# Sample rows join 96 prompt rows in the even portion of a hybrid decoder step, and the cache attention moves there

## The reference, cut to what matters

```
h  = rmsnorm(x) @ w_in                         # split into u, v, value and gate of glu, q, three gates
A  = gelu(u) * (tril(w_s) @ layernorm(gelu(v)) + b)       # in chunks of 128 rows; a sample chunk has 4 rows
B  = silu(layernorm(causal_depthwise_conv(glu, 31 taps))) # a sample starts from its conv state
M  = softmax(q @ mem_k) @ mem_v                # 4 heads of 256, 256 memory rows
x += (sig(gA) * (A @ w_oA) + sig(gB) * (B @ w_oB) + sig(gM) * (M @ w_oM)) @ w_out
x += peer(rmsnorm(x))     # 8 heads x top 16 of 128 x 128 product keys: dots with gathered u rows,
                          # then a weighted sum of the gathered v rows
```

## Time and profile before

| | |
|---|---|
| median of 3 runs | 2285.58 us (2284.76 to 2286.41) |
| profiled execution, its time | 2276.99 us |
| its span, first to last instruction | 2275.3 us |
| PE, DVE, ACT, POOL busy | 1634.6, 1574.6, 662.4, 669.7 us |
| moved by DMA | 895.53 MB, mean 394 GB/s |
| mean granted tensor clock | 0.798 |

### The profile page before, as it was taken

One profiled execution on the slowest core, in us unless ns is written; L12 is line 12 of the kernel. 1 busy time (PEld: TensorE's weight loads), 2 busy tenths in 40 slices (PEclk: granted clock), 3 DMA queues, 4 the chain that ended last, 5 costly groups with the idle time before them and its releaser, 6 DMA issues.

```text
span 2275.3 us, 31198 instructions
## 1 busy us (share of the span) xinstructions
PE 1634.6 (72%) x10876; PEld 1059.8 (47%) x10876; DVE 1574.6 (69%) x4199; ACT 662.4 (29%) x1662; POOL 669.7 (29%) x596
## 2 busy tenths in 40 slices
PE   8999977579897567788889647776999853334333
PEld 8865665357775145454534414643877620000001
DVE  3545288779756676877675567967865677776875
ACT  2112234321423242332123223342123233322222
POOL 0000032323332342333223233221322344444442
PEclk9999999779997678898889757877989865555555
DMA  8676899999999999999999999999999999999997
GB/s 297 267 289 251 295 391 421 420 421 408 412 420 420 421 421 420 422 401 417 421 381 423 421 421 409 415 409 406 414 375 412 392 393 422 422 421 421 421 421 310
DMA packets 127100, 895.53 MB, mean 394 GB/s; under 512 B 16065, under 2 KB 16897, under 8 KB 19169
## 3 DMA queue, kind: packets, MB, share of 16 engines
q0 software_dynamic: 83232, 604.02, 64.4%
q1 hardware_dynamic: 43712, 289.53, 31.9%
HBM read 885.38 MB, written 8.11 MB: 393 GB/s over the span
## 4 chain that ended last, share of the span: by engine, by line
DMA 34%; PE 29%; DVE 20%; issue 7%; ACT 4%; DVEq 3%; POOL 2%; SPq 0%; POOLq 0%; ACTq 0%
DMA uv<-uv_in,idx_u 24%; PE bank L1499 13%; DVE uv L1378 9%; DMA ring<-w_in 5%; PE bank L2005 4%; DMA ring<-cache_in 4%; PE bank L1505 4%; PE bank L1754 4%; DVE yB L964 3%; POOL uv L506 2%; DVEq L959 1%; ACT diag L881 1%; ACT L558 1%; DVE x L1399 1%; DVE pick L1343 1%
## 5 line engine op out<-in xcount | busy, mean ns | idle before, releaser
L506 POOL DMA_INDIRECT uv<-uv_in,idx_u x574 | 654.3, 1140 | 1381.0 <-PE bank L2005 933.4
L1378 DVE CUSTOM_DVE_ANT_0 uv<-uv,xrep 128x1024 f32<-128x1024 f32 x576 | 681.1, 1220 | 213.5 <-DMA uv<-uv_in,idx_u 211.9
L2005 PE MATMUL bank<-uv,diag 128*32 128x512 f32 x2176 | 401.0, 819 | 467.8 <-ACT diag L881 464.8
L1499 PEld LDWEIGHTS bank<-xnT,ring 128*128 128x128 f32 x3200 | 442.3, 204 | 81.2 <-issue 69.7
L1499 PE MATMUL bank<-xnT,ring 128*128 128x160 f32 (+1 forms) x3200 | 464.1, 306 | 6.7 <-DMA ring<-w_in 5.2
L558 ACT ACTIVATE pick<-pick 128x2 f32<-128x2 f32 (+1 forms) x324 | 69.6, 215 | 1062.0 <-DVE pick L1378 1061.4
L2005 PEld LDWEIGHTS bank<-uv,diag 128*32 128x32 f32 x2176 | 50.5, 124 | 658.3 <-ACT diag L881 594.9
L964 DVE SCALAR_TENSOR_TENSOR yB<-ext_p,small,yB 128x128 f32<-128x128 f32 x960 | 277.3, 350 | 20.4 <-issue 1.1
L558 ACT ACT_TABLE_LOAD x140 | 179.6, 1283 | 2.5
L881 ACT ACTIVATE diag<-gated_fold,pick 128x32 f32<-128x32 f32 x576 | 153.7, 314 | 9.6 <-ACT pick L558 0.2
L1754 PE MATMUL bank<-ring,xnT 128*128 128x512 f32 x192 | 89.6, 622 | 0.0
(11 more groups left out here) (228 smaller groups left out, 1769.9 us busy)
## 6 DMA issues: line engine op xcount, KB each, us to landing
ring<-w_in SPq DMA_DIRECT2D x216, 1024.0 KB, 9.8
ring<-cache_in SPq DMA_DIRECT2D x32, 1024.0 KB, 17.8
uv<-uv_in,idx_u POOLq DMA_INDIRECT x578, 16.4
uv<-w_in SPq DMA_DIRECT2D x4, 1024.0 KB, 13.4
ext_s<-state_in SPq DMA_DIRECT2D x2, 1088.0 KB, 13.7
convs_out<-ext_s SPq DMA_DIRECT2D x2, 1088.0 KB, 31.1
ext_s<-mem_in SPq DMA_DIRECT2D x2, 1024.0 KB, 14.9
memk_out<-phase SPq DMA_DIRECT2D x2, 1024.0 KB, 11.8
```

What stands on the lines that cost most here:

```text
L506: nc.gpsimd.indirect_dma_start(out=uvbuf[2 * b + i], out_offset=None, in_=uv_in, in_offset=bass.IndirectOffsetOnAxis(ap=ids[:, c:c + 1], a ...
L1378: ins = V.tensor_tensor_reduce(out=u, in0=u, in1=xrep[gg % 2][:, :], scale=1.0, scalar=0.0, op0=ALU.mult, op1=ALU.add, accum_out=hid[:, c: ...
L1499: ins = MM(out, w[:, k, P * b:P * (b + 1)], rhs(k), start=k == 0, stop=k == KB - 1)
L2005: ins = MM(vbank[gg % 2][c:c + 32, :], diag[:, t % 4, i], uvbuf[2 * b + i][:, D + 512 * n:D + 512 * (n + 1)], start=first, stop=last)
```

## The change

- The 32 sample rows go to the even portion, ahead of 96 prompt rows, so it has 128 columns as before. The odd portion has 160 prompt rows and no sample rows. The last 32 of them stand in the extra columns.
- The samples' convolution (state load, sample taps, store of the new state), their attention to the cache (ck, cv, sk, pts, sv, ot) and the store of their normalised v rows move to the even portion, with orders rewritten for all engines. There, q comes first, each mk or mv piece is followed by two cache pieces, and the prompt's own attention comes behind mv and sv, between the va pieces.
- In the odd portion the prompt's attention gets a fifth item for the 32 extra rows, all four heads in one (S4, T4, O4). The convolution runs over 160 columns there and over 96 in the even portion. The taps of the odd portion are handed out anew: three at each of the eight first mg places.
- A chunk of 128 rows of the spatial gate now lies across both portions. The masks are 160 columns wide, and the even portion keeps a partial sum (spart) for the odd one.
- The piece ua0 is kept for the odd portion like va3. The kept pieces now lie in the memory's and in the conv state's buffers, and are loaded when these come free.
- The expert scores have 9 slots instead of 10.

```diff
-SCORE_SLOTS = 10
+SCORE_SLOTS = 9
+SEQ_COLS = (slice(T_S, P), slice(0, P + T_S))
+SEQ_N = (P - T_S, P + T_S)
 def items(m):
+    kinds = [("glu", 0, 8), ("q", 0, 4)]
     if m % 2 == 0:
-        kinds = [("glu", 0, 8), ("mk", 0, 1), ("q", 0, 1), ("mk", 1, 2), ("q", 1, 2), ("mk", 2, 3), ("q", 2, 3), ("mk", 3, 4),
-                 ("mv", 0, 1), ("q", 3, 4), ("mv", 1, 4), ("va", 0, 4)]
-    else:
-        kinds = [("glu", 0, 8), ("q", 0, 4), ("va", 0, 3), ("ck", 0, 8), ("va", 3, 4), ("cv", 0, 8)]
+        for j in range(4):
+            kinds += [("mk", j, j + 1), ("ck", 2 * j, 2 * j + 2)]
+        for j in range(4):
+            kinds += [("mv", j, j + 1), ("cv", 2 * j, 2 * j + 2)]
+    kinds += [("va", 0, 4)]
...
-KEPT = [("va", 3)]
+KEPT = [("va", 3), ("ua", 0)]
...
     if p == 0:
...
+        out += some("q", h, *range(4))
+        out += some("mk", kv, 0) + some("sk", 2, 0, 1) + some("mk", kv, 1) + some("sk", 2, 2, 3)
+        out += some("mk", kv, 2) + some("pts", 0.8, 0) + some("sk", 2, 4, 5) + some("mk", kv, 3) + some("sk", 2, 6, 7)
+        out += some("mv", kv, 0) + some("pts", 0.8, 1) + some("sv", 2, 0, 1) + some("mv", kv, 1) + some("sv", 2, 2, 3)
+        out += some("mv", kv, 2) + some("sv", 2, 4, 5) + some("mv", kv, 3) + some("sv", 2, 6, 7)
+        out += some("va", across, 0) + S(0) + S(1) + [("ot", 0.8)] + some("va", across, 1) + T(0) + S(2) + some("va", across, 2)
+        out += T(1) + S(3) + T(2) + some("va", across, 3) + O(0) + O(1) + T(3) + O(2)
     else:
...
+        out += some("q", h, 0) + S(0) + some("q", h, 1) + S(1) + some("q", h, 2) + T(0) + S(2) + some("q", h, 3) + T(1) + S(3)
+        out += some("va", across, 0) + S(4) + O(0) + T(2) + some("va", across, 1) + O(1) + T(3) + some("va", across, 2) + O(2) + T(4)
+        out += some("va", across, 3) + O(3) + some("mg", h / 2, 0) + O(4) + some("mg", 3 * h / 2, 1)
...
-                    if p == 1 and (kind, i) == ("q", 3):
+                    if (kind, i) == ("q", 3):
                         sp.wait_ge(S["glu"], at("glu", m, 8))
...
# the even portion, vector engine
+                    yield from beside("q1", 1)
...
+                    yield from beside("mk0", 3)
...
+                    yield from beside("mv1", 4)
...
# the even portion, scalar engine: the exponentials stand behind the copies of mk2 and mv0
+                    for i in range(3):
+                        yield from mk(i)
+                    weigh_sample(0)
+                    yield from turned_sample(0)
+                    yield from mk(3)
+                    yield from mv(0)
+                    weigh_sample(1)
...
# the odd portion, vector engine
+                    yield from beside("va3", 3)
+                    yield from beside("O3", 2)
-                    yield from gated(0, 3, 2)
+                    yield from gated(0, 3, 3)
                     yield from norm_v_gain()
-                    yield from gated(3, 5, 2)
+                    yield from gated(3, 5, 3)
                     yield from norm_v_bias()
-                    yield from gated(5, 8, 2)
+                    yield from gated(5, 8, 3)
...
# convolve
+                            out, seq = yB[:, c, SEQ_COLS[p]], ext_p[:, c, w:w + SEQ_N[p]]
```

521 lines of the change are left out of this document (284 added, 237 removed).

## The result

After the change: 2317.40 us, median of 4 runs (2317.10 to 2318.67), against 2285.99 us for the kernel before on the same chip (2284.76 to 2288.14). The ratio is 1.0137, 95% interval 1.0120 to 1.0155: slower by 31 us. In two later sessions, on chips 2 and 13, the same kernel gave 1.0185 (1.0159 to 1.0211) and 1.0176 (1.0152 to 1.0201), some 40 us more than before. The forecast was +10.5 us. The direction was right, the size was not.

What follows compares the result with a forecast made beforehand. Tensor engine bounds up to the first gather, then the DMA stream, with the vector engine near it at the odd taps; +24 - 46.5 + 33 = +10.5 us, median 2296 us, range 2266 to 2320 (the forecast's own 2284 to 2310).

Steps and rivals of the forecast that it cites:

- Part 1: Stage before the first gather: layer 0's cache attention moves where the tensor engine binds and is paid, +24 us (17 to 32).
- the stated 0 to 4: First stage: possible waiting of 0 to 4 us for the cache pieces, requested at 355 GB/s with stores beside.
- Part 4: Costs nothing: even taps, extra prompt-row work, split-chunk copies, 9 score slots, later EARLY pieces, masks, stores of normalised rows.
- Part 2: Behind the first gather: 19.6 MB fewer bytes in the DMA stream, -46.5 us.
- Part 3: Odd portions: vector work of the taps exceeds DMA time and leaves DMA idle, +33 us (6 to 55).
- an excess of 36 to 38 us: Odd portions: vector time over DMA time from S4 to mg9, 36 and 38 us; the slots hide 15 to 17.
- what these places lose now: Odd portions before the change: 3.3 and 4.1 us of existing DMA loss, 7 in all, deducted from the added idleness.
- the 1.8 us of Part 4: Odd portion: time of O4's products, the out product for the last 32 prompt rows, taken to lie under the stream.
- (c): Rival: hard first stage, ring behind at mk and ck, +32, vector part at its upper bound; +40, 2326 us, chance 0.10.
- (a): Rival: odd portions' vector excess is hidden; -16, 2270 us, chance 0.24.
- (b): Rival: the edits cancel, 10 us more hidden in each stretch; 0, 2286 us, chance 0.16.
- (d): Rival: first-stage cache products hidden behind pieces the tensor engine would wait for anyway; given nothing of its own.

Runs made afterwards that it cites:

- e1: Changed kernel with the four early weight loads each issued behind a mixing load (mg12 to mg18) instead of all ahead of ua1; 1.0120 of the kernel before.
- e2: Changed kernel with 8 of each odd portion's tap steps moved from mg0 to mg7 into the glu phase; 1.0070 of the kernel before.
- f2: Changed kernel with one product of 256 columns in place of O4's 16 small ones, run beside a control; 1.0150 of the kernel before.
- e3: Changed kernel with 23 of the 62 tap steps of each odd portion left out; 0.9989 of the kernel before.
- e11: Changed kernel with e1, e2, e6, three more tap steps moved from va3 and O3 to glu, planner's cost of O4 5 instead of 1.2; 0.9973 of before.
- e4: Changed kernel with the planner's costs from va0 to sg3 of the odd portions 1.3 times as large; 1.0184 of the kernel before.
- e6: Changed kernel with 8 odd-portion tap steps moved from mg0 to mg7 to mg8 to mg11, csum and csq later; 1.0099 of the kernel before.
- f5: e11 plus cache-score turns one product pair later and one tap step fewer at each spatial product, one more at mg8 to mg11; 0.9957 of before.

## Why the prediction was right in sign and wrong in size

**Part 1, +24 (17 to 32) for the first stage: it was +41.5.** The walk up to gt0 was nearly right, 23.3 forecast for its terms and 28.2 measured; 3.4 of the rest is short waits for the ring, inside the stated 0 to 4, of which the sum took 0.4. What failed is a sentence of Part 4: the EARLY pieces "are fetched later, at ua0 instead of mv0, but over 100 us ahead of their first use", counted as nothing. It asked when the pieces are wanted, and not what stands behind them in the queue. ua1's load stood there: 4.36 us of waiting and 2.3 us at the lower level behind it, and e1 gets 6.7 us back with that one edit. The second step that failed is the clock, which has no term. The earlier trace rows showed 0.99 for a stage with hardly a wait, and it was taken to stay; the stage ran at 0.96. Rows at the lower level add some 6 us beside ua1's: O1 and O2 1.9, gt0 0.9, gt2 2.3 and the rows from 304.06 on 1.3. Part of them follows waits. gt2's does not: it is there in all six profiles without ua1's wait, and absent in two with it (e2 and f2). It stands behind the spatial products; why the level falls there is open.

**Part 2, -46.5: right.** 19.8 MB less. The even portion 2 kept 1.01 in the window shown, but not to its end: at 1148 us, in its knot of the prompt's attention, one window has 0.84, where the kernel before has none below 0.95 between 307 and 1587 us. That gap of 3 us is small, and it is one for which the forecast saw no cause.

**Part 3, +33 (6 to 55): it was +46.5, inside the bounds.** The mechanism was right: vector busy 0.89, gathers released late, dots never idle. The size of a step was right (37 against 34 ns for the width), and e3's 62% and e2's 57% are near the share that an excess of 36 to 38 us less 15 to 17 hidden leaves (57%), though the spread of the marks is wide. One reading was not: for the odd portion of layer 1 "what these places lose now" was taken from 1380 to 1500 us. Its first mg products stand from 1587 us on, and from 1560 to 1700 us the kernel before already ran at 394 GB/s, a loss of 9 us against 421.5 and not of 4. Two couplings are missing. One is O4: the 1.8 us of Part 4 measured 7.04, and 3.65 at full clock, in a corner where TensorE had waited 10.5 us. Without it some 6 us come back (5.9 by the ratios, not clear of the noise), in the second odd portion alone. The other is the granularity: the excess was summed over the whole stretch and set against slots, but slots are refilled one pair's values at a time, and in the corner two intervals of 14 to 17 us between values (va3 to mg1) meet a queue that brings no piece of the ring. e11 changes only where the pairs stand; it splits one of the two, and the corner's gap in the first odd portion all but closes. That e4, which leaves them as long, gains nothing fits this; it is not shown to be the reason. e2 and e6 take steps out of mg0 to mg7, and their gain needs no more than the excess.

**Part 4.** Right for the score slots, the masks, the copies and the even portions' taps, as far as no wait in the profile names them; not tried one by one. Wrong for EARLY and O4.

**Sum.** +10.5 became +41.6 by the span: +17.5 from the first stage and +13.5 from behind the first gather. The base makes a small difference more: the ratios of three sessions give 31 to 42 us.

**Rivals.** The text's own test, "if the first gather comes after 320 us (then c)", came true at 328.46. (c) had the ring behind at mk and ck; the ring did fall behind, but at ua1, and behind the first gather nearly the upper bound holds, as (c) has it. Its 2326 is 9 us above the result, and near what the ratios of the two later sessions give; the forecast's 2296 is 21 below. (a) is excluded by the share of 0.79 to 0.87, and (b) by the interval. (d) was rightly given nothing.

**What stays open.** How much of the first stage's +41.5 needs to stay: f5 still has its first gather 29 us later than before, of which some 16 are the cache's products and their turns. What takes the first stage's clock down at the spatial products. And the cause of the window some 800 us behind the first gather (0.82 in f5, 0.75 to 0.89 in the other versions).

## What to carry to other kernels

When a transfer is moved in a queue, price what stands behind it at the new place, not only the date of its own use. Where one engine's order interleaves long auxiliary work with the short work that frees a buffer, look at the longest intervals between two releases and at what else the queues can bring in them, not only at the sum over the stretch. Moving tap steps to places where the vector engine had room, spreading the early loads aside, with one planner cost took 42 us off the time behind the first gather, nearly as much as the bytes saved (46.5). And take a stage's granted clock as something that the change may move: here it fell behind waits of 4 to 10 us, and also at gt2, where there was none.

## What the runs showed of the hardware

- After a wait of 10.1 us TensorE did the next 8 value products in 1.94 us instead of 1.06, and the 16 gate products that followed 9 us later in 3.87 instead of 2.34. After waits of 3.75 to 5.01 us, 64 products took 8.75 to 10.33 us in eleven profiles, and 7.31 in the six without a wait.
- The clock also fell without a wait: in e1, after 42 us in which TensorE was busy without a gap and which end with the spatial products, the next 3.9 us were granted 0.50, and 16 products took 9.94 us instead of 7.13. The same place is slow in 15 of 17 profiles.
- 32 products of 32 columns, each with its own 128 x 128 weights, take 7.04 us at the lower level and 3.65 at the higher, 114 ns each. 32 products of 128 columns take 3.84 there: at so few columns the width no longer sets the time.
- A load of 1 MB that was issued behind five others on one queue was there 18.2 us after its issue, where the median of the kernel before is 4.9.
- The same kernel stands at 1.0137, 1.0176 and 1.0185 of its predecessor in different sessions, and its first gather varied from 327.3 to 330.0 us in three profiles.
